# Last round of the state-space mixer: the last group's decays ahead of two gate squares, low parts of y tiles 8 to 13 ahead of the last group's gates

## What is computed

```python
def mamba2_mixer(h, w_in, conv_w, conv_b, dt_bias, a_log, d_skip, gate_norm, w_out):
    z, xbc, dt = jnp.split(h @ w_in, [SSM_D_INNER, SSM_D_INNER + SSM_CONV_DIM], axis=-1)
    xbc = jax.nn.silu(causal_depthwise_conv(xbc, conv_w, conv_b))
    ...
    y = ssd_chunked(xs, dt, A, Bm, Cm) + d_skip.astype(f32)[:, None] * xs
    y = y.reshape(b, L, SSM_D_INNER) * jax.nn.silu(z.astype(f32))
    y = rmsnorm(y, gate_norm)
    return y.astype(h.dtype) @ w_out
```

## Time and profile before

| | us |
|---|---|
| three runs | 1898.51, 1901.17, 1902.83 |
| median | 1901.17 |
| the profiled execution, its own time | 1894.71 |
| its span in the trace, first to last instruction | 1892.9 |
| PE busy / DVE busy / POOL busy / ACT busy | 1843.7 / 1063.9 / 889.2 / 572.8 |
| mean granted clock of TensorE | 0.992 |

### The profile page before, as it was taken

One profiled execution on the slowest core, in us unless ns is written; L12 is line 12 of the kernel. 1 busy time (PEld: TensorE's weight loads), 2 busy tenths in 40 slices (PEclk: granted clock), 3 DMA queues, 4 the chain that ended last, 5 costly groups with the idle time before them and its releaser, 6 DMA issues.

```text
span 1892.9 us, 25043 instructions
## 1 busy us (share of the span) xinstructions
PE 1843.7 (97%) x9691; PEld 1469.2 (78%) x9691; DVE 1063.9 (56%) x1660; ACT 572.8 (30%) x1027; POOL 889.2 (47%) x902
## 2 busy tenths in 40 slices
PE   7999999989999999999999999999999999999998
PEld 5788888777777677478888888887777788888887
DVE  6888888975788664553333323257777733333212
ACT  4444445422344431242111100136654421111001
POOL 4444444444533345255555556544442455555553
PEclk9999999999999989999999999999999999999999
DMA  8776766667565379668888888886552588888875
GB/s 220 162 156 151 155 157 148 155 149 167 125 140 120 85 166 221 146 145 187 195 196 189 194 192 187 202 187 136 124 128 64 135 200 197 191 193 196 182 173 134
DMA packets 217317, 309.92 MB, mean 164 GB/s; under 512 B 22864, under 2 KB 171504, under 8 KB 217200
## 3 DMA queue, kind: packets, MB, share of 16 engines
q0 software_dynamic: 42912, 148.65, 45.8%
q1 hardware_dynamic: 169872, 154.28, 26.2%
q10 hardware_dynamic: 4416, 5.39, 1.1%
HBM read 153.12 MB, written 2.10 MB: 82 GB/s over the span
## 4 chain that ended last, share of the span: by engine, by line
PE 85%; DVE 8%; ACT 3%; issue 2%; DMA 1%; POOL 1%; SPq 0%; DVEq 0%; POOLq 0%; ACTq 0%
PE gp L731 23%; PE gp L733 22%; PE gp L732 22%; PE gp L671 2%; PE gp L672 2%; PE gp L678 2%; PE mp L999 1%; DVE m_xs L1882 1%; PE mp L1102 1%; PE gp L703 1%; DMA wl<-stage 1%; PE gp L705 1%; PE gp L704 1%; PE mp L871 1%; PE mp L965 1%
## 5 line engine op out<-in xcount | busy, mean ns | idle before, releaser
L619 POOL TENSOR_SCALAR wh<-stage 128x1024 fp32r<-128x1024 f32 (+3 forms) x300 | 348.9, 1163 | 886.4 <-PE gp L733 696.5
L731 PE MATMUL gp<-hh,wh 128*128 128x512 f32 x1504 | 602.5, 401 | 3.1 <-POOL wh L619 1.5
L732 PE MATMUL gp<-hh,wl 128*128 128x512 f32 x1504 | 587.2, 390 | 0.0
L733 PE MATMUL gp<-hl,wh 128*128 128x512 f32 x1472 | 575.2, 391 | 0.0
L625 POOL TENSOR_SCALAR wl<-stage 128x1024 fp32r<-128x1024 f32 (+2 forms) x298 | 351.2, 1179 | 0.0
L731 PEld LDWEIGHTS gp<-hh,wh 128*128 128x128 f32 x1504 | 283.3, 188 | 74.3 <-issue 18.0
L732 PEld LDWEIGHTS gp<-hh,wl 128*128 128x128 f32 x1504 | 283.5, 189 | 57.3 <-issue 1.4
L733 PEld LDWEIGHTS gp<-hl,wh 128*128 128x128 f32 x1472 | 277.0, 188 | 59.1
L628 POOL DMA_DIRECT2D wl<-stage x298 | 263.9, 886 | 94.7 <-POOL wl L625 86.3
L2313 DVE TENSOR_TENSOR val<-gp,rstd 128x512 f32<-128x512 f32 x44 | 30.4, 691 | 203.0 <-PE gp L733 203.0
L2206 DVE TENSOR_TENSOR xT<-gp,xT 128x512 f32<-128x512 f32 x31 | 21.4, 689 | 194.6 <-PE gp L733 189.8
(11 more groups left out here) (383 smaller groups left out, 2777.0 us busy)
## 6 DMA issues: line engine op xcount, KB each, us to landing
wl<-stage POOLq DMA_DIRECT2D x263, 512.0 KB, 5.3
stage<-ffn_w SPq DMA_DIRECT2D x120, 512.0 KB, 4.4
stage<-ssm_w_in SPq DMA_DIRECT2D x32, 512.0 KB, 5.1
stage<-hg_w_in SPq DMA_DIRECT2D x32, 512.0 KB, 4.6
stage<-ssm_w_in SPq DMA_DIRECT2D x32, 256.0 KB, 3.8
stage<-ssm_w_out SPq DMA_DIRECT2D x16, 512.0 KB, 4.2
stage<-att_w_in SPq DMA_DIRECT2D x14, 512.0 KB, 5.0
stage<-cp_w_in SPq DMA_DIRECT2D x12, 512.0 KB, 5.4
```

Of the source, the lines that this page charges most:

```text
L619: pool.tensor_scalar(wh[:, s, part], stage[:, s, part], 1.0, 1.0, ALU.mult, ALU.mult).then_inc(hi_done, 1)
L731: pe.matmul(bank[:, :], wvh[:, cols], hi(kk), start=start, stop=False)
L732: pe.matmul(bank[:, :], wvl[:, cols], hi(kk), start=False, stop=False)
L733: mm = pe.matmul(bank[:, :], wvh[:, cols], lo(kk), start=False, stop=stop)
```

## The change

```diff
-    y_split = [range(0, 8), range(8, 10), range(10, 12), range(0), range(12, 13), range(13, 14)]
+    y_split = [range(0, 8), range(8, 12), range(0), range(12, 14), range(0), range(0)]
...
                                 if g == SG and slot == 1:
                                     for k in y_split[slot]:
                                         high_y(k)
+                                if g == SG and slot == 2:
                                     gate_square(p - 1, 0)
                                     gate_square(p - 1, 1)
...
                         if g == SG and slot:
                             for k in y_split[slot]:
                                 low_y(k)
-                            if slot == 1:
+                            if slot == 2:
                                 gate_rest(p - 1, 0)
                                 gate_rest(p - 1, 1)
```

## The result

| | before | changed |
|---|---|---|
| median of the first comparison (10 runs each), us | 1899.64 | 1886.72 |
| ratio, 95% interval | | 0.9934 (0.9913 to 0.9955) |
| mean over the runs with a recorded clock (104 and 39), us | 1898.3 | 1888.0 |
| the profiled execution, its own time | 1894.71 | 1887.22 |
| its span | 1892.9 | 1885.4 |

The change is faster, and by more than forecast: 12.9 us in the first comparison, 10.3 +- 1.6 us over the runs of the second line, against 5.9. The 10 runs of before in the first comparison have a mean of 1900.1; their clocks were not recorded, so they are not among the 104, while the 10 of the changed kernel are among the 39.

The account below looks back on a forecast made before the run. PE was taken to bound the kernel, busy 97% of the span. Removing two waits for DVE's low parts, 3.07 + 2.84 = 5.9 us, from the median 1901.17 gave 1895.3 us, range 1891.3 to 1899.7.

Parts of the forecast that it names:

- The bound and the two stalls: PE bounds, 97% busy; in the first mixer's output projection it stands still 3.00 and 2.68 us for DVE's low parts.
- Parts 1 and 3: Low parts 10, 11 to slot 1: 3.07 us; group 6 gates behind products, then low parts 12, 13: 2.84.
- Part 2: ACT's decays ahead of the squares, ending at 379.9 and not 387.1 us; alone moves nothing on PE.
- Parts 3 and 4: Low part 12 ready with margin 3.1 us; `gate_sq` ahead of the sum of squares with 1.1 to 2.8 us.
- Rivals B and D: DVE late again beside POOL, 3.7 us gained, chance 0.12; only one stall goes, 3.07 gained, chance 0.07.
- Weights: POOL's passes in the stretch waited for PE, so weights were early; the next land at 403 us, costing nothing.
- the shift should be kept: No PE wait from 403.5 us to the projection's end; what follows is released by PE, so the gain lasts.
- Rival C: Clock's low stretch at the pause behind the projection 3 us longer or shorter: 4.4 or 7.4 us gained, chance 0.11.
- The sum's base: The 5.9 us gain was taken from the runs' median 1901.17, 6.5 us above the profiled execution, giving 1895.3.

Follow-up runs that it names:

- The table alone: Kernel before with only low and high parts 10, 11 moved to slot 1 and 12, 13 to slot 3, group 6 squares and gates unmoved: ratio 0.9946.
- the filled kernel: Kernel before with both stalls kept but filled by 12 and 11 unread matmuls: ratios 0.9988 and 0.9958, mean 1894.2 us.
- the runs with filled pauses: Changed kernel plus 10 unread matmuls in each of two pauses between the first three mixers: ratio to before 0.9955, mean 1886.8 us.

## Why the prediction was wrong

**The bound and the two stalls: right.** Both stalls were where DVE's order put them and both went. Parts 1 and 3 give 3.07 and 2.84, the trace 5.96 together.

**Part 2: right in direction, and without effect on PE**, as it said. The table alone shows that it was not needed.

**Parts 3 and 4, the margins: right.** Low part 12 was done ahead of need, the last gate waited 1.30 us for PE, `gate_sq` came about 397.1 against 399.73, 2.6 us of margin where 1.1 to 2.8 were forecast. Contention beside POOL took place (two products at 1.42 and 1.52 us, a gate's multiply at 1.41) and was covered. Not all of the moved work has two tiles as inputs, as the prediction says: the gate's scaled copy (L1954) has one, and it took 1.16 us beside the pass and 0.49 alone. Rivals B and D did not occur.

**Weights: right there.** PE had no wait behind the projection. Of the profiled gain 1.1 us was given back later: 8.62 us at the sum of squares, 7.5 us at the end, where waits for weights by DMA in the changed profile came to 5.1 us against 2.4, 1.3 of these ahead of the change. So "the shift should be kept" was too strong, though these waits go with the early start rather than with the change: they are 1.3 to 3.2 us in the seven profiles that start late, two of them with the change, and 3.2 to 6.6 in the seven that start early, three of them without it.

**Rival C, the clock: the step that failed.** The prediction said: "The two stalls removed did not lower the clock (1.00 from 389.5 to 403.5), so nothing is won there." That is true of the profiled execution and not of the kernel. The stalls lower the clock in other executions; the clock lost over all runs and the filled kernel put the price at 3.5 +- 1.0 and 4.1 +- 1.7 us in the mean, about as much as either stall's own length, where the sum had nothing. A single slow stretch behind a stall made the work 1.4 to 1.6 us longer. The Trainium skill, page "TensorE: Matmul & The Clock Gate", section "HAM oscillation — how this bites in real kernels", describes a kernel whose TensorE falls back to the low clock at its waits between bursts of matmuls; two gaps of 3.0 and 2.7 us bore that out in one profile here and not in another of the same program. What failed was to take one clean trace for the rule. The pauses of rival C do vary by chance: the two profiles of the filled kernel, one program, lie in the two groups above, 2.4 us apart.

**The sum's base: a clue that was passed over.** "1901.17, 6.5 us above the profiled one; the same 5.9 us from it" took the difference for noise around one behaviour. The profiled execution was one in which an effect of the very stalls was missing. 5.9 + 3.5 is 9.4, inside the 10.3 +- 1.6 that was measured; it would have given 1891.8 from the median of three. The clock is thus the largest part of the miss, not all of it. The 8.6 us between 1895.3 and 1886.72 are 3.5 of clock, 1.0 more of time without the clock, 2.8 by which the median of three lay above the mean of before (1898.3), and 1.3 by which the median of the first comparison lay below that of all runs of the changed kernel (1888.0). The last two are luck.

**What stays open.** The first comparison had 12.9 us; that and the 10.3 of all runs agree within their errors. The time without the clock fell by 6.9 +- 1.0, the trace has 5.96: the difference may be the start of the run, with its unrecorded clock, or nothing. And the profiles show fewer slow stretches behind the stalls than 3.5 us would need.

## What to carry to other kernels

A stall of TensorE costs more than its idle time when the clock falls with it, and whether it does can differ between executions of one program, so a clock of 1.00 in one profile does not price it. Before forecasting from one profiled execution, ask what the distance between its time and the median consists of, and compare its mean clock with that of the other runs. In order-bound code, look for results that have been ready for long and stand in a queue behind a wait for the very engine that needs them.

## What the runs showed of the hardware

- The clock fell to 0.50 at stalls of 2.99 and 2.67 us in one execution and stayed at 1.00 at 3.00 and 2.68 in another of the same program; in all profiles it fell at three of seven such stalls, for 3.4 us each, and made the work behind 1.4 to 1.6 us longer.
- 23 matmuls that nobody reads, put in the stalls, took 4.1 +- 1.7 us off the kernel.
- Clock lost in a pause is not all time lost: between two groups of profiles 3.4 us of it went with 2.4 us of time, and over the runs with filled pauses 6.4 us less of it with 1.2 +- 2.3.
- At the start of an execution TensorE can be slow where the record shows 1.00: the same seven matmuls took 3.12 us in one profile and 1.70 in another.
- Executions of one program differ by some 4 us already in the first 75 us, by the clock there and by whether DVE instructions meet a POOL pass (0.68 us alone, up to 3.54 beside one).
